# Encoder layers with chunked attention: scores laid out in whole key tiles, masks folded into the keys

## The reference

```
def _fox_attend(q, k, v, c_q, c_k, pos_q, pos_k):
    s = einsum('bqhd,bkhd->bhqk', q, k) * HD_B ** -0.5
    s = s + (c_q[..., :, None] - c_k[..., None, :])
    s = where(pos_k[None, :] <= pos_q[:, None], s, -inf)
    return einsum('bhqk,bkhd->bqhd', softmax(s), v)

def _dsa_attend(q, k, v, iq, ik, iw, cid_q, cid_k, k_top):
    score = einsum('bqhk,bqh->bqk', relu(einsum('bqhd,bkd->bqhk', iq, ik)), iw) * IDX_SCALE
    score = where(cid_k[None, :] <= cid_q[:, None], score, -inf)
    sel = top_k(score, kk)                      # 256 keys for each query
    s = einsum('bqhd,bqsd->bqhs', q, k[sel]) * HD_C ** -0.5
    s = where(valid, s, -inf)
    return einsum('bqhs,bqsd->bqhd', softmax(s), v[sel])
```

## Time and profile before

| | |
|---|---|
| median of 3 runs | 2261.97 us (2259.77 to 2267.71) |
| profiled execution | 2242.35 us, its span 2240.4 us |
| mean granted clock of PE | 0.963 |
| busy: PE, DVE, ACT, POOL | 2069.9, 1483.6, 641.7, 325.3 us |
| attention of the first layer | about 556 to 841 us of the span |
| attention of the second layer | about 1664 to 1951 us |

### The profile page before, as it was taken

The page is one execution under the profiler, slowest core; times in us unless marked ns, Lnnn a source line. Parts: engine busy times, 40 slices in busy tenths (PEclk is TensorE's granted clock), DMA queues, the critical chain, the costliest instruction groups (busy, mean ns, idle before and its releaser), DMA issues. The chain is left out here.

```text
span 2240.4 us, 27372 instructions
## 1 busy us (share of the span) xinstructions
PE 2069.9 (92%) x9906; PEld 1273.2 (57%) x9930; DVE 1483.6 (66%) x3125; ACT 641.7 (29%) x1478; POOL 325.3 (15%) x418
## 2 busy tenths in 40 slices
PE   3999999998999996999969999999989999979997
PEld 3644444446776775666445444444467777756663
DVE  3256999999454545877333579999975545468871
ACT  3334000101333333444143430011023333334441
POOL 0000000000000004656200000000000000146651
PEclk9999999999999996999979999999989999879999
DMA  7221132222102202233051212311130022022321
GB/s 278 81 68 35 67 118 75 75 68 72 33 8 88 81 1 104 69 104 108 38 187 53 66 67 83 108 65 59 58 80 20 6 92 76 32 74 76 118 87 59
DMA packets 144006, 169.95 MB, mean 76 GB/s; under 512 B 68560, under 2 KB 106192, under 8 KB 143600
## 3 DMA queue, kind: packets, MB, share of 16 engines
q1 hardware_dynamic: 118400, 135.52, 19.0%
q10 hardware_dynamic: 25472, 32.66, 4.1%
HBM read 115.53 MB, written 62.50 MB: 79 GB/s over the span
## 5 line engine op out<-in xcount | busy, mean ns | idle before, releaser
L767 PE MATMUL ps<-wring,xnT_arena 128*128 128x512 f32 (+3 forms) x2304 | 883.0, 540 | 0.0
L767 PEld LDWEIGHTS ps<-wring,xnT_arena 128*128 128x128 f32 x2304 | 430.7, 190 | 431.4 <-issue 369.4
L1485 DVE TENSOR_SCALAR_CACHE_REDUCE arena<-arena,theta 32x1056 bf16<-32x1056 f32 x496 | 471.5, 987 | 8.8
L1573 DVE TENSOR_REDUCE small<-ps 128x1 f32<-128x192 f32 (+9 forms) x148 | 114.0, 770 | 152.1 <-PE ps L942 145.4
L1178 ACT COPY arena<-ps 128x512 f32<-128x512 f32 (+2 forms) x96 | 51.2, 533 | 464.4 <-PE ps L767 464.4
L1470 DVE SCALAR_TENSOR_TENSOR arena<-arena,iw 128x512 f32<-128x512 f32 (+6 forms) x224 | 135.7, 606 | 57.3 <-ACT arena L1233 50.5
L1065 PEld LDWEIGHTS ps<-arena 128*128 128x128 f32 x632 | 102.6, 209 | 102.5 <-DVE arena L1673 51.7
L1065 PE MATMUL ps<-arena 128*128 128x128 f32 (+1 forms) x632 | 124.7, 330 | 38.9 <-DVE arena L1673 32.5
L1009 PE MATMUL ps<-wring,arena 128*128 128x512 f32 x320 | 152.6, 607 | 5.7 <-DVE arena L1614 5.7
L1326 ACT ACTIVATE arena<-ps,small 128x192 f32<-128x192 f32 (+9 forms) x148 | 111.0, 750 | 156.6 <-DVE small L1573 156.5
L1009 PE MATMUL ps<-wring,xnT_arena 128*128 128x512 f32 x256 | 118.3, 593 | 0.0
(11 more groups left out here) (239 smaller groups left out, 2526.0 us busy)
## 6 DMA issues: line engine op xcount, KB each, us to landing
wring<-in_w_in SPq DMA_DIRECT2D x24, 1024.0 KB, 7.6
projected<-arena ACTq DMA_DIRECT2D x96, 256.0 KB, 2.0
arena<-residual SPq DMA_DIRECT2D x36, 512.0 KB, 5.2
arena<-projected SPq DMA_DIRECT2D x36, 384.0 KB, 3.8
arena<-projected SPq DMA_DIRECT2D x18, 512.0 KB, 6.2
residual<-arena SPq DMA_DIRECT2D x18, 512.0 KB, 2.7
wring<-in_w_out SPq DMA_DIRECT2D x8, 1024.0 KB, 7.4
out<-arena SPq DMA_DIRECT2D x16, 512.0 KB, 3.9
```

What stands on the lines that cost most here:

```text
L767: o = mm(bank(pbank(k), 0, wide), xnT[:, c, t * P:(t + 1) * P], w, start=(c == 0), stop=(c == CH - 1))
L1485: V.tensor_scalar(cmp_out[r, (i % 2) * WMAX:(i % 2) * WMAX + uw[u]], score[u][r], th_, 0.0, op, ALU.add, accum_out=into[r, i:i + 1]).then_ ...
L1573: V.tensor_reduce(mneg[:, s:s + 1], ps[:, base + lo:base + hi], X, ALU.max, negate=True).then_inc(a_max, 1)
```

## The change

Tile 0 now counts as a whole key tile of 128 columns, in the keys (`foxKT`, `dsaKT`), in the scores and in the penalty, so a job of tile t has 128 + 128t columns, and they begin at the first column of the job's first bank. Its columns that are no keys are hidden by a value in row 64 of the keys: for fox POOL writes -1e30 into the forget sums `negc`, and for dsa into row 64 of `dsaKT` (queries have a constant in row 64, left there by fox). So `nometa` is gone. `dsaown` is kept only for tile 1, since the penalty of tiles 2 to 8 already excludes these keys; for tile 2, which has fewer admissible keys than 256, DVE writes -1e30 over the block by hand. The index scores, and with them `keep`, stay in the old layout, so for each of the units 2 to 8 DVE now writes the penalty in pieces: a 64-column `tensor_scalar`, a 64-column memset, a wait from unit 3 on, and a `tensor_scalar` of the remaining columns (unit 2: also a wait and a 64x64 memset). The transposed keys of dsa are copied in one piece where there were two. In the sample unit the 32 new keys come last instead of first. The runs of tiles 0 to 8 go from 1, 2, 2, 2, 2, 3, 3, 3, 3 to 1, 1, 1, 1, 2, 2, 2, 2, 3.

```diff
--- before.py
+++ after.py
@@ -61,6 +61,10 @@
 
 def width(t):
     return HALF + P * t
+
+
+def key_width(t):
+    return P + P * t
 
 
 SW = PAST + NS
@@ -112,7 +116,6 @@
     b["rep"] = rep
     b["causal"] = -BIG * gt.T
     b["dsaown"] = -BIG * ((r[:, None] < 64) & (r[None, :] >= 64))
-    b["nometa"] = np.repeat(-BIG * (np.arange(HALF) < SMETA)[None, :], P, 0)
     c0 = np.arange(HALF)
     meta_row = (r >= SMETA) & (r < HALF)
     b["foxmeta"] = np.where(meta_row[:, None] & (c0[None, :] >= SMETA) & (c0[None, :] <= r[:, None]), 0, -BIG)
@@ -232,8 +235,10 @@
         uw = {"s": SW, **{t: width(t) for t in range(2, NT)}}
         score = {u: cut([uw[u]]) for u in UNITS}
 
-        pen = {u: score[u].bitcast(BF16)[:, 0:uw[u]] for u in UNITS}
-        relu = [cut([WMAX]) for _ in range(2)]
+        penw = {"s": SW, **{t: key_width(t) for t in range(2, NT)}}
+        pen = {u: score[u].bitcast(BF16)[:, 0:penw[u]] for u in UNITS}
+        WK = key_width(NT - 1)
+        relu = [cut([WK]) for _ in range(2)]
         idxtok = cut([NT, NIX])
         ikT = cut([WMAX + NS])
         ikTs = cut([SW])
@@ -251,16 +256,16 @@
         idxc = cut([NCACHE, DI])
 
         ca = carve(xnT_arena, CH * NT * P)
-        foxKT = ca([H, WMAX])
+        foxKT = ca([H, WK])
         foxV = ca([NT, H * HD])
         ptile = [ca([NT * P]) for _ in range(2)]
         pbuf = relu
 
-        cn_at = sum(uw.values()) + 2 * WMAX
+        cn_at = sum(uw.values()) + 2 * WK
         stage_at = cn_at + NT * NIX + WMAX + NS + SW + 2 * NI * P + 4 * D
         foxVs = arena[:, stage_at - NT * H * HD:stage_at].rearrange("p (a b) -> p a b", a=NT)
         cn = carve(arena[:, cn_at:], stage_at - NT * H * HD - cn_at)
-        dsaKT = {"p": cn([WMAX]), "s": cn([SW])}
+        dsaKT = {"p": cn([WK]), "s": cn([SW])}
         dsaKV = cn([NT, 2 * HD])
         dsaKc = cn([NCACHE, HD])
         dsaVc = cn([NCACHE, HD])
@@ -413,8 +418,8 @@
 
             m, u = mu
             if u == "s":
-                return [(PAST, NS, 512 - NS)] + [(j * P, P, 512 + j * P) for j in range(NCACHE)]
-            return [(0, HALF, 512 - HALF)] + [(HALF + P * j, P, 512 + P * j) for j in range(u)]
+                return [(j * P, P, j * P) for j in range(NCACHE)] + [(PAST, NS, PAST)]
+            return [(P * j, P, P * j) for j in range(u + 1)]
 
         def span(mu):
             cols = [(c, w) for _, w, c in pieces_of(mu)]
@@ -926,9 +931,10 @@
                                     adds.append((CB("rep")[0:NS, :], pen["s"][0:NS, key:key + w], 0, w))
                             else:
                                 if key == 0:
-                                    own = {"fox": "foxmeta", "dsa": "dsameta"}[m] if u == 0 else "nometa"
-                                    adds.append((CB("identb"), CB(own), 0, HALF))
-                                if u > 0 and key + w == width(u):
+                                    own = {"fox": "foxmeta", "dsa": "dsameta"}[m]
+                                    if u == 0:
+                                        adds.append((CB("identb"), CB(own), 0, HALF))
+                                if u > 0 and key + w == key_width(u) and (m == "fox" or u == 1):
                                     adds.append((CB("identb"), CB("causal" if m == "fox" else "dsaown"), w - P, P))
                                 if m == "dsa" and u >= 2:
                                     adds.append((CB("identb"), pen[u][:, key:key + w], 0, w))
@@ -970,9 +976,9 @@
                             o0 = 7 * 512
                             if u == "s":
                                 if m == "fox":
-                                    o = mm(ps[:, o0:o0 + 256], pt, foxVs[0:w, i - 1 if i else NCACHE, :], start=(i == 0), stop=(i == len(ch) - 1), skip_group_check=True)
+                                    o = mm(ps[:, o0:o0 + 256], pt, foxVs[0:w, i, :], start=(i == 0), stop=(i == len(ch) - 1), skip_group_check=True)
                                 else:
-                                    v = dsaVc[:, i - 1, :] if i else dsaKV[0:NS, 0, HD:2 * HD]
+                                    v = dsaVc[:, i, :] if i < NCACHE else dsaKV[0:NS, 0, HD:2 * HD]
                                     o = mm(ps[:, o0:o0 + HD], pt, v, start=(i == 0), stop=(i == len(ch) - 1), skip_group_check=True)
                             else:
                                 v = foxV[0:w, i, h * HD:(h + 1) * HD] if m == "fox" else dsaKV[0:w, i, HD:2 * HD]
@@ -1106,17 +1112,14 @@
                     b = tbank[a]
                     if m == "fox":
                         rows = NS if u == "s" and j == NCACHE else P
-                        col = (P * j if u == "s" else max(0, width(u - 1))) if u != 0 else 0
-                        n_ = HALF if u == 0 else rows
+                        col = P * j if u == "s" else P * u
+                        n_ = rows
                         return copy(foxKT[0:HD + 1, :, col:col + n_], ps[0:HD + 1, 512 * b:512 * b + 512].rearrange("p (h n) -> p h n", h=H)[:, :, 0:n_])
                     if u == "s":
                         n_ = min(SW - P * j, 4 * P)
                         return copy(dsaKT["s"][0:HD, P * j:P * j + n_], ps[0:HD, 512 * b:512 * b + n_])
-                    if j == 0:
-                        copy(dsaKT["p"][0:HD, 0:HALF], ps[0:HD, 512 * b:512 * b + HALF]).then_inc(own_sem, one_more(own))
-                        return copy(dsaKT["p"][0:HD, HALF:HALF + 3 * P], ps[0:HD, 512 * b + P:512 * b + 4 * P])
                     n_ = min(NT - j, 4) * P
-                    return copy(dsaKT["p"][0:HD, width(j - 1):width(j - 1) + n_], ps[0:HD, 512 * b:512 * b + n_])
+                    return copy(dsaKT["p"][0:HD, P * j:P * j + n_], ps[0:HD, 512 * b:512 * b + n_])
 
                 def copy_p(copy, a, te):
 
@@ -1529,7 +1532,18 @@
                         dve.wait_ge(dve_own, own[0])
                         V.tensor_tensor(keep, keep, equal, ALU.add).then_inc(dve_own, one_more(own))
                         dve.wait_ge(dve_own, own[0])
-                        o = V.tensor_scalar(pen[u][r], keep, 0.0, -BIG, ALU.is_equal, ALU.mult)
+                        if u == "s":
+                            o = V.tensor_scalar(pen[u][r], keep, 0.0, -BIG, ALU.is_equal, ALU.mult)
+                        else:
+                            V.tensor_scalar(pen[u][:, 0:HALF], keep[:, 0:HALF], 0.0, -BIG, ALU.is_equal, ALU.mult).then_inc(dve_own, one_more(own))
+                            V.memset(pen[u][:, HALF:P], 0.0).then_inc(dve_own, one_more(own))
+                            if u > 2:
+                                dve.wait_ge(dve_own, own[0])
+                            o = V.tensor_scalar(pen[u][:, P:penw[u]], keep[:, HALF:w], 0.0, -BIG, ALU.is_equal, ALU.mult)
+                            if u == 2:
+                                o.then_inc(dve_own, one_more(own))
+                                dve.wait_ge(dve_own, own[0])
+                                o = V.memset(pen[u][0:HALF, penw[u] - HALF:penw[u]], -BIG)
                         o.then_inc(pen_done, 1)
                         dve.wait_ge(pen_done, pen_done_at[u])
 
@@ -1733,6 +1747,9 @@
                     for i in range(4):
                         nc.gpsimd.memset(QT[i][HALF:], 0.0).then_inc(pool_own, one_more(own))
                     pool.wait_ge(pool_own, own[0])
+                    nc.gpsimd.memset(dsaKT["p"][HALF:HALF + 1, 0:SMETA], -BIG).then_inc(pool_own, one_more(own))
+                    nc.gpsimd.memset(dsaKT["p"][HALF:HALF + 1, HALF:P], -BIG).then_inc(pool_own, one_more(own))
+                    pool.wait_ge(pool_own, own[0])
                     nc.gpsimd.memset(small[:, 87:88], 0.0).then_inc(pad_rest, 1)
                     pool.wait_ge(pad_rest, 1)
                     pool.wait_ge(ld_fox, 32)
@@ -1754,6 +1771,9 @@
                     pool.wait_ge(pool_own, own[0])
                     nc.gpsimd.memset(small[:, 85:86], 0.0).then_inc(lf_run, 1)
                     pool.wait_ge(lf_negc, 1)
+                    nc.gpsimd.memset(negc[0:SMETA, NCACHE + 1], -BIG).then_inc(pool_own, one_more(own))
+                    nc.gpsimd.memset(negc[HALF:, NCACHE + 1], -BIG).then_inc(pool_own, one_more(own))
+                    pool.wait_ge(pool_own, own[0])
                     for n, k in enumerate(FKS):
                         if n == NKA:
                             pool.wait_ge(p_mm, p_mm_at[jobs[-1]])
```

## The result

The changed kernel takes 2234.2 us (median of 4 runs, 2217.07 to 2244.71) beside 2260.87 us for the kernel before: ratio 0.9867, 95% interval 0.9819 to 0.9915. Run twice more beside the kernel before, it gave 0.9831 (0.9797 to 0.9866) and 0.9889 (0.9848 to 0.993). It is 1.1 to 1.7% faster, some 27 to 38 us. I had forecast no change, 2262 us, and a range down to 2254.5.

A forecast was written before the change was run, and what follows sets the result against it. PE bounds the attention, except group [0, 4], and DVE the stretch before it; per layer -3.1 + 0.6 + 1.7 + 0.11 + 0.6 = -0.1 us, -0.2 for two, so 2262 us, range 2254.5 to 2270.

The forecast's parts named there:

- The step that failed: PE in attention groups [1, 5] to [8]: transposes, value matmuls and copies of four tiles change by nothing.
- Part 1: PE in attention groups [1, 5] to [8]: fewer, longer score runs and fewer masks give -3.1 us per layer.
- Rival C: PE in the attention gains by number of records, not columns: 17 us per layer, 2228 us; chance 0.05.
- PE stays full from group [1, 5] on: Sign in the attention's changed profile: PE has no new gaps there, and the attention is some 2.5 us shorter.
- the 0.12 us a job that I had called covered: Groups [1, 5] to [8]: maximum grows 0.067 us and exponential 0.053, covered by other jobs' PE work.
- Part 2: Attention group [0, 4]: longer turns through tile 4's scores, maximum and exponential cost +0.6 us per layer.
- Part 3: DVE ahead of the attention: split penalty writes +1.7 us per layer, larger clearing memset +0.11, longer stall +0.6.
- The stall: Ahead of the attention, unit 7's DVE tensor_scalars stand still 1.6 to 1.9 us for POOL's memset: +0.6 us per layer.

The follow-up runs named there:

- e7: Changed kernel with 64 rows in all value matmuls of the prompt, half of the values of each key tile left out; 2258.83 us in a single run.
- e1: Changed kernel, but the value matmul of tile 0 takes 64 rows again; 2261.29 us, ratio 0.9987.
- e3: Kernel before, with only the value matmul of tile 0 taking all 128 rows; 2241.45 us, ratio 0.9891.
- a3: Changed kernel again, unaltered, for another profile; median 2232.11 us (6 runs).
- e5: Changed kernel, but POOL clears both halves of the padding of foxKT, beginning at the last scan, and DVE no longer clears; 2220.22 us, ratio 0.9817.
- e2: Changed kernel with value matmuls of 64 rows and transposes of 64 columns for tile 0; 2260.78 us.

## Why the prediction was wrong

**The step that failed** is the sentence "Transposes and value matmuls keep their number, their 128 and 64 moving columns, and the copies of four tiles their size: nothing." The value matmul of tile 0 had 64 rows, and stepping from 128 rows to 64 and back costs PE 0.28 to 0.34 us a job (e7, e1). I counted instructions and columns and overlooked the shape in front of them. The trace of before showed it: eight value records at 0.11 are 0.88 us, and they took 1.08. e1 and e3 settle it from both sides, -14 us per layer if only this is done and +13 if only this is undone, of the 18 us that the attention got shorter. In the time e3 makes 1.1% of this.

**Part 1, scores**: the right mechanism, about half of the size. Per job it is -0.07 instead of -0.04 (tile 3, 1.04 to 0.97); from e3 to the changed kernel the attention gets 3 to 5 us per layer shorter, 5 in the first layer at clock 1.00 (273.5 to 268.5 in a3), where parts 1 and 2 together had 2.5.

**Rival C**, time by number of records, is not what happened. Its 2228 us lie near the measured 2234.2 by chance: in e3 all the masks are still there and most of the gain is made, and the run of 64 columns with `nometa` still costs 0.25 us in it, as before.

**"PE stays full from group [1, 5] on"** was wrong. In the changed kernel PE waits for ACT's exponential before the transposes, which is this line of the waits over both layers (total us, times, longest us):

```profile
PE ps L960 <- ACT arena L1329: 9.5, 22, 0.7
```

It was 0.8 us in 4 waits before. The turn of [1, 5] went only from 5.41 us (604.79 to 610.20) to 5.19 (608.28 to 613.47) where [3, 7] gained 0.78. A faster PE there meets the latency of maximum and exponential, which got longer by the 0.12 us a job that I had called covered. That fits the 13 to 14 us that came of the 22 us that the values give back to PE; no run separates it further.

**Part 2** was right: a turn went from 4.65 to 4.74 us, and I had forecast +0.09.

**Part 3** was right. DVE's clearing memset begins 10.51 - 8.14 = 2.37 us later after POOL's, forecast 1.7 + 0.6. The stall is 2.02 - 0.18 = 1.84 us, at the instruction that I had named. e5 shows the cause: with POOL's memset beside the scan there is no stall. This agrees with the lock that the Trainium skill describes (SBUF — State Buffer, Who interferes with whom). The memset of 64 bf16 columns took 0.09 us instead of 0.11; the trace shows it as 32 columns of uint32.

**The sum** from the pieces is: the attention -16 and -20 us, DVE ahead of it 2.4 later in each layer, PE's end 0.4 later (546.19, 545.80), together -31. Measured over the runs it is -27 to -38. The stretches that the clock moves are left out of this sum.

**The base.** I noted that the profiled execution stood 19.6 us under the median and put the same change on both. That was sound, but had I compared two single executions I would have found no gain at all.

## What to carry to other kernels

Read the shape in front of an instruction, not only its count and its columns: among full matmuls one with fewer rows cost more than itself here, and padding it with zeros to the full height was one line for 1.1%. The rows that meet the zeros must hold finite numbers. If a profiled execution and the runs disagree, compare stage by stage and look at the granted clock of the stages that the change does not touch. When an in-order engine gets faster in a pipeline of jobs, ask which group of jobs has the least slack; there the gain is likely to end.

## What was not expected of the hardware

Matmuls with 64 rows, once the step is made, cost no more and no less than full ones: the records follow at 0.11 us in e7 as in the changed kernel, and the Trainium skill says so of the load (TensorE: Matmul & The Clock Gate, LDWEIGHTS: the time goes by columns, not by rows). What it does not say there is the gap at the step between heights, 0.20 us from start to start instead of 0.11, with a second, smaller delay behind it (0.16), in both directions. A step between widths (e2) costs nothing that can be seen.

The stage behind the attention took 289 to 308 us in eleven profiles of kernels that have the same code there, in no relation to the edit that could be seen (289.3 before, 290.5 in e1, 305.2 in e2, 307.5 and 293.8 in the changed kernel), with a granted clock of 0.92 to 0.88 in the middle of the four shown. It alone can make more difference between two executions than half of this change.
